# Gate blocks moved between the column groups of the input projection, and a top-256 search issued pass by pass

## What is computed

```
xn = rmsnorm(x)
z  = xn @ w_in       # columns: nsa q, k/v (cmp, slc, win), nsa gates, dsa q, k, v, indexer q, k, weights, 2048 merge gates
score = sum_h iw_h * relu(iq_h . ik)        # indexer, causal
dsa   = attention of each query over its 256 highest-scoring keys
nsa   = g0 * compressed + g1 * selected blocks + g2 * sliding window
merged = sigmoid(z_gA) * (nsa @ w_branch_nsa) + sigmoid(z_gB) * (dsa @ w_branch_dsa)
h = x + merged @ w_out
out = rmsnorm(h + swiglu(rmsnorm(h)))
```

## Time and profile before

| | |
|---|---|
| median of 3 runs | 1877.56 us |
| lowest, highest | 1875.97, 1878.3 us |
| span of the profiled execution | 1870.0 us |
| own time of that execution | not given; the median is 7.6 us over the span |
| TensorE busy, share of the span | 1777.7 us, 95% |
| VectorE, ScalarE, GpSimd busy | 45%, 36%, 31% |
| mean granted TensorE clock | 0.985 |

### The profile page before, as it was taken

The page is one execution under the profiler, slowest core; times in us unless marked ns, Lnnn a source line. Parts: engine busy times, 40 slices in busy tenths (PEclk is TensorE's granted clock), DMA queues, the critical chain, the costliest instruction groups (busy, mean ns, idle before and its releaser), DMA issues.

```text
span 1870.0 us, 25106 instructions
## 1 busy us (share of the span) xinstructions
PE 1777.7 (95%) x9596; PEld 1526.2 (82%) x9596; DVE 837.2 (45%) x1796; ACT 672.4 (36%) x1310; POOL 584.2 (31%) x366
## 2 busy tenths in 40 slices
PE   6789979999999999999999989999999999999997
PEld 5667768888898999899988878888888888888886
DVE  6689788999135545566646322111131012311102
ACT  5543333221355467655522023322222223222222
POOL 3303233221220011321122024454454444544541
PEclk9899999999999989999999999999999999999999
DMA  5103232532422001001044223333333333433331
GB/s 175 45 12 103 80 96 86 174 90 74 113 64 113 24 29 30 12 17 31 1 130 141 80 85 96 91 100 103 90 102 102 101 90 90 140 105 93 101 102 68
DMA packets 179462, 158.01 MB, mean 84 GB/s; under 512 B 16912, under 2 KB 145936, under 8 KB 179088
## 3 DMA queue, kind: packets, MB, share of 16 engines
q1 hardware_dynamic: 179344, 156.41, 27.4%
HBM read 131.22 MB, written 25.17 MB: 84 GB/s over the span
## 4 chain that ended last, share of the span: by engine, by line
PE 84%; DVE 8%; ACT 3%; issue 2%; POOL 2%; DMA 1%; SPq 0%; DVEq 0%; ACTq 0%; POOLq 0%
PE psA L1075 18%; PE psA L1077 18%; PE psA L1076 18%; PE psT L1257 9%; PE psT L1082 7%; PE psA L1142 3%; PE psA L1141 3%; PE psT L1075 2%; PE psT L1077 2%; PE psT L1076 2%; POOL w_lo L319 1%; DVE rotated L1474 1%; DVE equal L1534 1%; DVE above L1534 1%; PE psT L1266 1%
## 5 line engine op out<-in xcount | busy, mean ns | idle before, releaser
L319 POOL TENSOR_TENSOR w_lo<-w_raw,w_hi 128x1024 fp32r<-128x1024 f32 (+2 forms) x184 | 453.6, 2479 | 657.4 <-ACT w_hi L314 657.4
L314 ACT CAST w_hi<-w_raw 128x1024 fp32r<-128x1024 f32 (+2 forms) x184 | 186.6, 1038 | 660.4 <-PE psA L1077 525.9
L1075 PE MATMUL psA<-hTh,w_hi 128*128 128x512 f32 x704 | 273.9, 389 | 0.2 <-POOL w_lo L319 0.2
L1076 PE MATMUL psA<-hTl,w_hi 128*128 128x512 f32 x704 | 273.9, 389 | 0.0
L1077 PE MATMUL psA<-hTh,w_lo 128*128 128x512 f32 x704 | 273.9, 389 | 0.0
L1820 DVE TENSOR_TENSOR act<-silu,psA 128x512 f32<-128x512 f32 x44 | 30.2, 687 | 393.5 <-ACT silu L1046 393.5
L971 ACT ACTIVATE p<-s,nmax 128x640 f32<-128x640 f32 (+7 forms) x192 | 144.0, 750 | 120.3 <-DVE nmax L1647 119.1
L1075 PEld LDWEIGHTS psA<-hTh,w_hi 128*128 128x128 f32 x704 | 132.1, 188 | 28.2 <-issue 0.6
L1076 PEld LDWEIGHTS psA<-hTl,w_hi 128*128 128x128 f32 x704 | 132.1, 188 | 27.4
L1077 PEld LDWEIGHTS psA<-hTh,w_lo 128*128 128x128 f32 x704 | 132.1, 188 | 27.2
L1082 PE MATMUL psT<-ident,p 128*128 128x128 f32 x816 | 131.0, 281 | 18.8 <-DVE yTl_dsa L1706 4.7
(11 more groups left out here) (259 smaller groups left out, 3544.4 us busy)
## 6 DMA issues: line engine op xcount, KB each, us to landing
w_raw<-in_w_gate_dram SPq DMA_DIRECT2D x44, 512.0 KB, 3.8
w_raw<-in_w_up_dram SPq DMA_DIRECT2D x44, 512.0 KB, 3.9
w_raw<-in_w_down_dram SPq DMA_DIRECT2D x44, 512.0 KB, 3.8
w_raw<-in_w_in_dram SPq DMA_DIRECT2D x28, 512.0 KB, 3.9
scratch_gates<-gate_out SPq DMA_DIRECT2D x32, 256.0 KB, 2.9
gates<-scratch_gates SPq DMA_DIRECT2D x32, 256.0 KB, 4.1
xr<-in_x_dram SPq DMA_DIRECT2D x8, 512.0 KB, 4.9
scratch_q_dsa<-turned SPq DMA_DIRECT2D x8, 512.0 KB, 2.6
```

The costliest lines, as they stand in the source:

```text
L314: nc.scalar.copy(self.hi[n % RING][:, 0:u], self.raw[n % RAW][:, 0:u]).then_inc(self.hi_done, 1)
L319: nc.gpsimd.tensor_tensor(self.lo[n % RING][:, 0:u], self.raw[n % RAW][:, 0:u], self.hi[n % RING][:, 0:u].bitcast(F32), ALU.subtract).then ...
L1075: pe.matmul(ps, ah, bh, start=first, stop=False)
L1076: pe.matmul(ps, ah, bl, start=False, stop=False)
```

## The change

The gate blocks are spread: none behind `idx`, three blocks (six gate steps) behind each of `qb`, `cmp` and `win`, and seven (14 gate steps) behind `qa`. One list `main` of column steps ("z") and gate steps ("g") drives the loops of all engines. A step n of a kind stands at position `pos_of[kind, n]`, its PSUM bank is that position modulo 4, and `free1` and the waits for ring slots are derived from the list. `z_turn(q)` now always follows the step behind q+1, also at the end. The search is issued in single passes: `bisect(n)` does pass n % 6 of round n // 6, two passes behind each column step and five behind each gate step, 186 in all, and the building and keeping of the bit stand with the first and the last pass of a round. The last 32 passes fall behind step 39.

```diff
-    items1 = sum((chunk_items(w_in, *COLS[c]) for c in ORDER), [])
-    NCH = len(items1)
-    items1 += [[(w_in[:, :, o_gm + P * j:o_gm + P * (j + 1)], 0, KT, P)] for j in range(2 * KT)]
+    GATES_AFTER = {IDX: 0, QB: 3, CMP: 3, WKV: 3, QA: 7}
+    items1, main, chunk_at, gate_at = [], [], {}, []
+    for ch, c in enumerate(ORDER):
+        chunk_at[ch] = len(items1)
+        items1 += chunk_items(w_in, *COLS[c])
+        main += [("z", NT * ch + i) for i in range(NT)]
+        for _ in range(GATES_AFTER[c]):
+            j = len(gate_at)
+            gate_at.append(len(items1))
+            items1.append([(w_in[:, :, o_gm + P * j:o_gm + P * (j + 1)], 0, KT, P)])
+            main += [("g", 2 * j), ("g", 2 * j + 1)]
+    pos_of = {step: n for n, step in enumerate(main)}
...
+    free1 = [0] * len(items1)
+    for ch, n in chunk_at.items():
+        free1[n:n + 4] = [pos_of["z", NT * ch + NT - 1]] * 4
+    for j, n in enumerate(gate_at):
+        free1[n] = pos_of["g", 2 * j + 1]
...
+        last_z = pos_of["z", Z_STEPS - 1]
+        for at_, (kind, n) in enumerate(main):
+            for item in w1.due(at_, RAW + RING):
+                w1.load(sp, item)
+            if kind == "g":
+                sp.wait_ge(g_out, n + 1)
+                sp.dma_start(gD[n // 2, :, HALF * (n % 2):HALF * (n % 2 + 1)], gst[n % 2][:])\
+                    .then_inc(g_stored[n % 2], 16)
+            if at_ >= 3 and main[at_ - 3][0] == "z":
+                spill(main[at_ - 3][1])
+            if at_ == last_z + 5:
...
+        for at_, (kind, n) in enumerate(main):
+            for item in w1.due(at_, RING):
+                w1.split_lo(pool, item)
+            if kind == "z":
+                rope_cos(n)
...
+        def stage2():
+            for at_ in range(NT, len(main)):
+                for n in w1.due(at_, RING):
+                    w1.split_hi(act, n)
+                kind, n = main[at_]
+                (z_evac if kind == "z" else gate_evac)(n)
+                if main[at_ - 1][0] == "z" and at_ > NT:
+                    block_hi(main[at_ - 1][1])
+                if main[at_ - 2][0] == "z" and at_ > NT + 1:
+                    turned_out(main[at_ - 2][1])
...
+        def gate_step(g):
+            n, half = gate_at[g // 2], slice(HALF * (g % 2), HALF * (g % 2 + 1))
+            pe.wait_ge(w1.lo_done, n + 1)
+            pe.wait_ge(*bank_out(pos_of["g", g] - 4))
+            hi, lo = w1.parts(n, KT)
+            three(psA[:, pos_of["g", g] % 4, :], [((hi[:, k, :], lo[:, k, :]), (xTh[:, k, half], xTl[:, k, half]))
+                                                  for k in range(KT)]).then_inc(g_ps, 1)
+        def stage2():
+            for at_ in range(NT, len(main)):
+                kind, n = main[at_]
+                (z_step if kind == "z" else gate_step)(n)
+                if main[at_ - 2][0] == "z" and at_ > NT + 1:
+                    z_turn(main[at_ - 2][1])
...
-            if g in (1, 2, 3):
-                z_turn(Z_STEPS - 4 + g)
...
+        def bisect(n):
+            bit, at_ = 30 - n // NTK, n % NTK
+            if at_ == 0:
+                then(v_.tensor_scalar(bit_try[:, R], bit_cur[:, R], 1 << bit, None, ALU.bitwise_or))
+                then(v_.tensor_tensor(bit_try[:, R], bit_try[:, R], bit_flip[:, R], ALU.bitwise_xor))
+            else:
+                dve.wait_ge(dve_seq, counted[n - 2 if at_ > 1 else n - 1])
+            counted.append(signal(v_.tensor_scalar((tk_gt, tk_eq)[at_ % 2][:, 0:P * (TK[at_] + 1)], score_of(TK[at_]),
+                                                   bit_try[:, at_:at_ + 1].bitcast(F32), None, ALU.is_ge, ALU.add,
+                                                   accum_out=count[:, at_:at_ + 1])))
+            if at_ == NTK - 1:
+                dve.wait_ge(dve_seq, counted[n])
+                then(v_.tensor_scalar(bit_keep[:, R], count[:, R], float(TOPK), float(1 << bit), ALU.is_ge, ALU.mult))
+                then(v_.tensor_tensor(bit_cur[:, R], bit_cur[:, R], bit_keep[:, R], ALU.bitwise_or))
...
-        for q in range(NT, Z_STEPS + 1):
-            if q < Z_STEPS:
-                rope(q)
-            if q > NT:
-                block_lo(q - 1)
-            if q % 2 == 0 and bit >= 0:
-                bisect(bit)
-                bit -= 1
-        while bit >= 0:
-            bisect(bit)
-            bit -= 1
+        counted, passes, in_step = [], 31 * NTK, {"z": 2, "g": 5}
+        for at_ in range(NT, len(main)):
+            if main[at_][0] == "z":
+                rope(main[at_][1])
+            if main[at_ - 1][0] == "z" and at_ > NT:
+                block_lo(main[at_ - 1][1])
+            for n in range(len(counted), min(passes, len(counted) + in_step[main[at_][0]])):
+                bisect(n)
...
```

More of the change, by code:

```diff
@@ L454, in hybrid_block @@
     gD = scratch["gates"]
[L457 to L462, removed]
+    w1.gone = [None] * len(items1)
+    for ch, n in chunk_at.items():
+        w1.gone[n:n + 4] = [(w1.freed, 3 * ch + a + 1) for a in range(3)] + [(z_ps, 8 * ch + 8)]
+    for j, n in enumerate(gate_at):
+        w1.gone[n] = (g_ps, 2 * j + 2)
     w2.gone = [(m_ps, 2 * j + 2) for j in range(KT)]
@@ L552, in spill @@
             sp.dma_start(dst, src.bitcast(F32)).then_inc(spilled[n % 2], 16)
-        for q in range(Z_STEPS + 3):
-            if q < Z_STEPS:
[L556 to L559, removed]
         def load_q(k):
@@ L881, in turned_out, with gate_evac @@
                 last.then_inc(zt_out, 1)
[L883 to L892, removed]
+        def gate_evac(g):
+            act.wait_ge(g_ps, g + 1)
+            if g >= 2:
+                act.wait_ge(g_stored[g % 2], 16 * (g // 2))
+            a_.activation(gst[g % 2][:], psA[:, pos_of["g", g] % 4, :], ACT.Sigmoid).then_inc(g_out, 1)
+        def stage2():
[8 more added lines that the diff above has]
+                    turned_out(main[at_ - 2][1])
         def id_relu(v):
@@ L927, in _ @@
         act.wait_ge(id_ps, len(iunits))
[L928 to L935, removed]
+        stage2()
         for u in range(STEPS6):
@@ L1099, in x_turn, with bank_out @@
                     .then_inc(xt_ps, 1)
+        def bank_out(at_):
+            kind, n = main[at_]
+            return (z_out if kind == "z" else g_out), n + 1
         def z_step(q):
@@ L1103, in z_step @@
             width = COLS[c][1]
-            if q >= 4:
-                pe.wait_ge(z_out, q - 3)
+            if pos_of["z", q] >= 4:
+                pe.wait_ge(*bank_out(pos_of["z", q] - 4))
             if q == NT:
@@ L1114, in z_step @@
                 hi, lo = w1.parts(n, 2)
-                mm = three(psA[:, q % 4, 0:width],
+                mm = three(psA[:, pos_of["z", q] % 4, 0:width],
                            [((xTh[:, 2 * a + k, tok(i)], xTl[:, 2 * a + k, tok(i)]), (hi[:, k, :], lo[:, k, :]))
@@ L1169, in _ @@
             id_unit(v)
-        stage2(NT, Z_STEPS)
-        for g in range(G_STEPS):
-            if g in (1, 2, 3):
-                z_turn(Z_STEPS - 4 + g)
[L1174 to L1179, removed]
-            hi, lo = w1.parts(n, KT)
-            three(psA[:, g % 4, :], [((hi[:, k, :], lo[:, k, :]), (xTh[:, k, half], xTl[:, k, half]))
-                                     for k in range(KT)]).then_inc(g_ps, 1)
+        stage2()
         pe.wait_ge(g_out, G_STEPS)
```

20 lines of the change are left out of this document (2 added, 18 removed).

## The result

The changed kernel takes 1881.09 us (median of 20 runs, 1875.62 to 1886.61), the kernel before 1876.33 in the same 20 rounds (1867.19 to 1881.93). The ratio is 1.0026 with a 95% interval of 1.0016 to 1.0037. The difference is 4.8 us; 6.7 were forecast. The forecast time, 1884.3 us, was 3.2 us too high: 1.9 of it in the difference, and 1.2 in the starting point, since it was added to a median of three runs (1877.56) that lay above that of the 20. The interval of the ratio leaves no room for "no change", though 1881.09 lies inside the band that the prediction called the same (1873.8 to 1881.3).

A forecast was written before the change was run, and what follows sets the result against it. TensorE, busy for 95% of the span, was taken as the bound. The terms 10.7 - 5.2 + 1.0 + 0.2 gave +6.7 us, added to the median 1877.56: 1884.3 us, range 1872 to 1891.

The forecast's parts named there:

- waits at the ends of qb, cmp, win, qa: TensorE waits for blocks before transposes, one gate step behind each group: 6.2, 4.3, 6.3 and 6.5 us, sum 23.3.
- clock lost behind them: TensorE's clock falls to 0.50 behind each of the four group-end waits, costing 1.6 us each, 6.4 in all.
- waits for low halves left: TensorE's waits for w_lo from GpSimd fall from 10.0 us to under 2 us.
- term 2: Search spread to two passes a step: VectorE's late blocks in win and two waits elsewhere go, -5.2 us.
- term 3: In win, VectorE needs 3.6 us a step against TensorE's 3.67 and starts late: +1.0 us, between 0 and 3.
- gate steps back to columns: Where columns follow gate steps, the fourth weight split is late under a thin cover: +0.2 us, 0 to 1.
- selection ends before the last gate is out: VectorE's selection ends near 400 against the last gate at 403.6: cost 0, bound +2.2 us.
- main step: At group ends the change leaves the chain of loads, splits and low halves unchanged; only the consumer, now a gate step, changes.
- term 1: Four group-end waits with their clock loss, 29.7 us against 19.0 before: +10.7 us.
- Rival (a): The four group-end waits shrink to some 3 us without a clock drop: 1866.6 us; chance 0.15.
- Rival (b): Group-end waits as forecast, but clock not lost or blocks ready a little earlier: 1877.9 us, no change; chance 0.2.
- Rival (c): Selection becomes the bound on top of the four waits, and VectorE bounds win: some 1889 to 1893 us; chance 0.1.

The follow-up runs named there:

- e7: Changed kernel with 81 useless matmuls added on TensorE, in the first gate step behind each column group: 1875.15 us, ratio 0.9989 to the kernel before.
- e3: Kernel before with only the search spread out, two single counting passes per column step and the rest behind the last: 1874.71 us, ratio 0.9980.
- e4: Changed kernel with two of four weight splits and low halves moved behind the work of each group's last step: 1855.99 us, ratio 0.9882 to the kernel before.
- e6: Changed kernel with 16 of the 31 search rounds, the lower 15 bits not searched: 1883.33 us, ratio 1.0024 to the kernel before.
- e2: Changed kernel with the transposes of the last two steps of qa one gate step later: 1880.51 us, ratio 1.0017 to the kernel before.
- e5: Kernel before with two of four weight splits and low halves moved behind the work of each group's last step: 1876.37 us, ratio 0.9996.
- e1: Changed kernel with the transposes of the last two steps of every group one gate step later: 1871.77 us, ratio 0.9969 to the kernel before.

## Why the prediction was right, and by how much each step was off

Measured values are from the profile of the changed kernel unless an experiment is named.

| Step of the prediction | Forecast | Measured |
|---|---|---|
| waits at the ends of qb, cmp, win, qa | 6.2, 4.3, 6.3, 6.5 us | 6.23, 3.99, 5.11, 6.25 |
| clock lost behind them | 6.4 us | 7.6 by the rows, 6 to 7 by e7 |
| waits for low halves left | under 2 us | 0.94 |
| term 2, waits that the spread search removes | 5.2 us | all five gone (e3 too) |
| term 3, waits inside win | 1.0 us | none |
| gate steps back to columns | 0.2 us | none |
| selection ends before the last gate is out | within 3 us, or 3.6 by its sum (near 400, and 403.6) | 3.6 (497.1 and 500.7) |
| difference of the stretch | +6.7 us | +5.4 |
| difference of the medians | +6.7 us | +4.8 |

**The main step held.** It was that the change moves the consumer and leaves the chain, so that waits for `w_lo` turn into waits for `blocks` at the same places. e4 shows it by cutting the chain, e6 by taking the counting passes from the engine that the wait names, and e7 by filling the idle time without moving its end.

**What was mis-sized.** Two terms were too high: term 3 (1.0 us) and the one for the gate steps back to columns (0.2) measured nothing. Term 3 came from a balance of 3.6 us of VectorE against 3.67 of TensorE in a step of `win`, with a microsecond of lateness to start with; the measured group has no wait at all. For the other the prediction called a cover thin that by its own numbers was 0.5 us (1.05 + 2.49 against 4.1). Inside term 1 two errors of the opposite sign nearly cancelled, which is luck: the four waits with the 0.94 us for a low half at the end of `win` came to 22.5 us instead of 23.3, and the clock cost 7.6 instead of 6.4. With these, 22.5 + 7.6 - 19.0 - 5.2 makes 5.9 us, against 5.4 measured in the stretch.

The clock term was one figure, 1.6 us, for every wait. The runs show 1.4 to 3.0 behind the four waits, and none behind the 3.12 us of e3, so its total came out near by averaging and not by a rule for a single wait.

**Rival (a)** said that the waits shrink to some 3 us each. The four rows above rule it out, and e6 rules out that VectorE's load sets their length. **Rival (b)**, the clock not lost, is ruled out by e7. **Rival (c)**, the selection as the bound, did not come true but was near: 3.6 us were left of 27, and in e2 it came true, with the last gate 5.6 us earlier and the end of the selection 4.5 later in its execution. The prediction did not see how much could be had: it looked for the price of the new waits and did not ask what would remove them. With the chain cut the same change gains 21 us.

## What to carry to other kernels

- Ask of every wait which chain it hangs on, not which buffer it names. If a change moves only the consumer, the wait moves with it; here 10 us for one buffer became 13 us more for another.
- In an engine that works in order, work that may wait for a DMA load belongs behind the work that others wait for. In the changed kernel, two splits moved behind an evacuation, and their low halves behind a cosine product, were worth 25 us, where the change alone cost 5. In the kernel before, the same move was worth nothing (e5).
- A waiting engine with a clock that falls pays twice, and the cover on the other engines is used up silently: look at what ends next (here the selection, 3.6 us) before counting a gain.

## What the runs showed of the hardware that was not expected

The loss of clock did not follow the length of the wait. It was 1.5 and 1.4 us behind the waits of 6.23 and 6.25 us, but 3.0 behind the one of 5.11. What differed is when the clock fell. These are the four stretches at the lower level, with their waits in them:

```profile
172.70:179.70 7.00, 2.85 (x11) 2.66 (x12) 6.96 (x10) 3.35 (x5) 2.49 (x2) 0.52 0.90 291
265.30:268.50 3.20, 3.20 (x10) 2.52 (x9) 3.16 (x11) 0.86 (x2) 0.00 (x0) 0.50 0.74 240
333.40:340.20 6.80, 5.99 (x16) 4.89 (x17) 6.56 (x21) 1.08 (x3) 0.00 (x0) 0.50 0.68 202
422.50:428.90 6.40, 2.90 (x11) 2.71 (x12) 6.37 (x10) 1.33 (x3) 1.83 (x2) 0.50 0.94 291
```

In the first and the last the clock fell some 4 us ahead of the end of the wait, and most of the low stretch was idle time that cost nothing more. In the third it fell 0.8 us ahead of that end, and nearly all of it was work at half speed. In the second it fell when TensorE had been at work again for 0.8 us. And a wait of 3.12 us (e3) had no fall behind it, where 3.04 (the kernel before) and 2.75 (e1) had one. Useless matmuls in the waits made the kernel faster by 6 us, e7.

The collisions of VectorE and GpSimd vary with small shifts in time. Operations of 0.17 us took 2.39 and 1.87 in the tail of e2, and none of their kind took over 0.77 in the tail of the changed kernel. A margin of 3 us that rests on them is none.
